# Splits made in place in the output stage, identity products on TensorE at the start of stages, and another order of loads and roundings in an encoder block on one Trainium2 core

## The reference

```python
ada = silu(c) @ w_ada + b_ada                     # six vectors of 1024
u = x * (1 + sc1) + sh1
p_h, p_qkv, p_gate = split(u @ w_in)              # one projection, 1024 -> 5888
y_h = hyena_mixer(p_h, ...)                       # long convolution by transforms
y_a = attention_mixer(p_qkv, positions)           # 3 dilations x 4 heads x 64
gate_h, gate_a = split(sigmoid(p_gate))
merged = gate_h * (y_h @ w_branch_hyena) + gate_a * (y_a @ w_branch_attn)
x = layer_norm(alpha * x + (1 + g1) * (merged @ w_out))
u2 = x * (1 + sc2) + sh2
f = peer(u2, wq, keys, utab, vtab)                # 8 heads, 16384 experts, best 16 per head
x = layer_norm(alpha * x + (1 + g2) * f)
```

## Time and profile before

| | |
|---|---|
| median of 3 runs | 3749.43 us (3746.46 to 3751.86) |
| the profiled execution's own time | 3747.55 us |
| its span | 3745.7 us |
| TensorE busy | 3526.9 us, 94% of the span |
| VectorE, GpSimd, ScalarE busy | 69%, 35%, 34% |
| mean granted clock of TensorE | .975 of full speed |

### The profile page before, as it was taken

How to read it: one execution, slowest core, us unless ns; L and a number is a source line. 1 busy time by engine, 2 the same in 40 slices (tenths; PEclk the granted TensorE clock), 3 DMA queues, 4 the chain that set the end, 5 groups by cost and what they waited for, 6 DMA issues and landing times. The chain is left out here.

```text
span 3745.7 us, 52511 instructions
## 1 busy us (share of the span) xinstructions
PE 3526.9 (94%) x18656; PEld 3116.3 (83%) x18656; DVE 2593.1 (69%) x5904; ACT 1291.3 (34%) x2645; POOL 1317.8 (35%) x815
## 2 busy tenths in 40 slices
PE   5699899999989799999999999999899999999997
PEld 4599788877767688999999999999788888888886
DVE  6663245435654555899988878888488777778877
ACT  2110232221142312322237888888322222222222
POOL 1232122213312112586652222222145555555532
PEclk9799999999999899999999999999999999999999
DMA  5353322327652223588757999999988888888873
GB/s 208 118 161 99 124 86 86 110 86 264 206 180 85 74 67 109 191 291 271 266 199 244 281 271 291 272 274 282 268 307 301 304 302 301 303 316 307 307 271 118
DMA packets 497846, 805.50 MB, mean 215 GB/s; under 512 B 289318, under 2 KB 304455, under 8 KB 494952
## 3 DMA queue, kind: packets, MB, share of 16 engines
q1 hardware_dynamic: 111432, 351.94, 26.9%
q0 software_dynamic: 85520, 311.47, 23.8%
...
...
## 5 line engine op out<-in xcount | busy, mean ns | idle before, releaser
L2451 POOL DMA_INDIRECT va_rows<-in_vtab,k_pick x256 | 481.2, 1880 | 526.0 <-DVE k_big L2629 403.7
L79 PE MATMUL va_fps<-va_vt_h,va_c_h 128*128 128x512 f32 x1536 | 600.5, 391 | 22.1 <-DVEq L2699 8.9
L80 PE MATMUL va_fps<-va_vt_l,va_c_h 128*128 128x512 f32 x1536 | 599.6, 390 | 0.0
L81 PE MATMUL va_fps<-va_vt_h,va_c_l 128*128 128x512 f32 x1536 | 599.5, 390 | 0.0
L2629 DVE SCALAR_TENSOR_TENSOR k_big<-va_rows,k_dots,k_big 128x1024 f32<-128x1024 f32 x254 | 317.8, 1281 | 73.9 <-DMA va_rows<-in_vtab,k_pick 73.9
L79 PEld LDWEIGHTS va_fps<-va_vt_h,va_c_h 128*128 128x128 f32 x1536 | 289.8, 189 | 83.9 <-DVEq L2699 9.3
L2264 ACT ACTIVATE ga_first<-ga_first,ga_gs 128x128 f16<-128x128 f16 x1152 | 355.9, 392 | 0.0
L81 PEld LDWEIGHTS va_fps<-va_vt_h,va_c_l 128*128 128x128 f32 x1536 | 289.7, 189 | 60.5
L80 PEld LDWEIGHTS va_fps<-va_vt_l,va_c_h 128*128 128x128 f32 x1536 | 289.9, 189 | 59.9
L2542 ACT ACTIVATE va_vt_h<-k_edge 128x1024 fp32r<-128x1024 f32 x128 | 135.5, 1058 | 555.7 <-PE va_fps L81 350.9
L2328 DVE TENSOR_SCALAR ga_second<-ga_iota,k_sel 128x128 f16<-128x128 f16 x768 | 201.0, 265 | 107.0 <-PE ga_ps L2226 85.0
...
## 6 DMA issues: line engine op xcount, KB each, us to landing
k_ut<-in_utab SPq DMA_DIRECT2D x128, 512.0 KB, 4.4
k_edge<-in_vtab SPq DMA_DIRECT2D x128, 512.0 KB
scratch_ahead<-k_gelu_a ACTq DMA_DIRECT2D x128, 384.0 KB, 2.7
k_edge<-scratch_ahead SPq DMA_DIRECT2D x128, 384.0 KB
k_edge<-scratch_gates SPq DMA_DIRECT2D x128, 384.0 KB
...
```

Source lines behind the costliest of these rows:

```text
L79: nc.tensor.matmul(out, w[0], x[0], start=first, stop=False)
L80: nc.tensor.matmul(out, w[0], x[1], start=False, stop=False)
L81: return nc.tensor.matmul(out, w[1], x[0], start=False, stop=last)
L2451: nc.gpsimd.indirect_dma_start(got[:, q % SLOTS_G, :], None, vrows, picked(K, q)).then_inc(got_in[q % SLOTS_G], 16)
```

## The change

- `keep_busy(count)` issues plain float32 products of the identity with itself into a PSUM tile that is overwritten later: 24 at the start of qkv, 16 at the start of mix and 14 at its end, 32 at the start of merge, 9 of out, 12 of values.
- setup: the load of `c` stands earlier in its queue, and the wait for the other small loads stands in spectra on VectorE.
- mix: VectorE, not GpSimd, makes the low part of the first weight tile.
- merge: the loads of weight tile 0 stand ahead of that of `y`, GpSimd rounds the weights as well as subtracting, ScalarE rounds `wo` before the sigmoid, VectorE subtracts `wo` before it gates, `wo` is loaded two tiles ahead, and TensorE waits for four `y` tiles and later for six.
- out: `m_h` and `m_l` live in the memory of `k_u_h` and `k_u_l`. When token tile n is turned, ScalarE rounds it into `k_u_h` over `m_h` of that tile, and VectorE subtracts three rows later. VectorE makes `m_l` of tile 0, GpSimd the other seven. There are three row buffers and two of statistics, the roots run two tiles ahead, and rows are stored from SP's queue. The first query weights are loaded here.
- query: no splits of `u2`. VectorE makes the low part of the first weights. `k_u_h` and `k_u_l` are laid out by token tile, so a moving operand is read as four runs of 128 (three in the 384-column products).

The diff, cut to its core (of the products, the forms in query and select stand for the others):

```diff
+def keep_busy(nc, out, K, count):
+
+    for _ in range(count):
+        nc.tensor.matmul(out, K["ident"][:, :], K["ident"][:, :], start=True, stop=True)
...
+            keep_busy(nc, tps[:, 0, 0:P], K, 24)
...
                 nc.gpsimd.tensor_copy(w_h[:, c % 2, :, :], w[:, :, :]).then_inc(w_hi, 1)
+                if c == 0:
+                    continue
                 pool.wait_ge(w_hi, c + 1)
+                pool.wait_ge(w_ok, c)
                 nc.gpsimd.tensor_tensor(w_l[:, c % 2, :, :], w[:, :, :], w_h[:, c % 2, :, :].bitcast(F32),
                                         ALU.subtract).then_inc(w_ok, 1)
...
+            keep_busy(nc, tps[:, 0, 0:P], K, 16)
             for m in lead:
                 project(m)
...
+            keep_busy(nc, sps[:, 0, 0:P], K, 14)
...
+            dve.wait_ge(w_hi, 1)
+            v.tensor_tensor(w_l[:, 0, :, :], w[:, :, :], w_h[:, 0, :, :].bitcast(F32), ALU.subtract).then_inc(w_ok, 1)
...
+            load_w(0)
             sp.dma_start(K["ya"], S["ya"]).then_inc(ya_in, 16)
-            with sp.Fori(0, KT // 2) as i:
-                for s in range(2):
-                    n = 2 * i + s
-                    sp.wait_ge(w_ok, n + 1)
-                    sp.dma_start(w[:, s, 0:NH, :], T["w_bh"][bass.ds(n, 1)][0]).then_inc(w_in[s], 16)
-                    sp.dma_start(w[:, s, NH:NY, :], T["w_ba"][bass.ds(n, 1)][0]).then_inc(w_in[s], 16)
-                    sp.wait_ge(m_ok, n + 1)
-                    sp.dma_start(gate[:, s, 0, :], S["cm"][bass.ds(HY_TILES + n, 1)][0]).then_inc(g_in[s], 16)
-                    sp.dma_start(gate[:, s, 1, :], S["cm"][bass.ds(HY_TILES + KT + n, 1)][0]).then_inc(g_in[s], 16)
-                    sp.wait_ge(wo_lo, n + 1)
-                    sp.dma_start(wo[:, s, :], T["w_out"][:, bass.ds(n, 1), :][:, 0, :]).then_inc(wo_in[s], 16)
+            load_w(1)
+            load_gate(0)
+            load_wo(0)
+            load_gate(1)
+            load_wo(1)
+            for n in range(2, KT):
+                load_wo(n)
+                load_w(n)
+                load_gate(n)
...
-            pool.sem_inc(w_ok, 2)
-            with pool.Fori(0, KT // 2) as i:
-                for s in range(2):
-                    pool.wait_ge(w_hi, 2 * i + s + 1)
-                    nc.gpsimd.tensor_tensor(w_l[:, s, :, :], w[:, s, :, :], w_h[:, s, :, :].bitcast(F32),
-                                            ALU.subtract).then_inc(w_ok, 1)
+            for n in range(KT):
+                pool.wait_ge(w_in[n % 2], 32 * (n // 2 + 1))
+                if n >= 2:
+                    pool.wait_ge(mm, 2 * n + 2)
+                nc.gpsimd.tensor_copy(w_h[:, n % 2, :, :], w[:, n % 2, :, :]).then_inc(w_hi, 1)
+                pool.wait_ge(w_hi, n + 1)
+                nc.gpsimd.tensor_tensor(w_l[:, n % 2, :, :], w[:, n % 2, :, :], w_h[:, n % 2, :, :].bitcast(F32),
+                                        ALU.subtract).then_inc(w_ok, 1)
...
+            keep_busy(nc, ps[:, 0, 0:P], K, 32)
...
                     for a, (lo, hi) in enumerate(((0, NH), (NH, NY))):
+                        pe.wait_ge(y_lo, hi)
...
-                    act.wait_ge(w_in[s], 32 * (i + 1))
-                    act.wait_ge(mm, 2 * n + 2)
-                    nc.scalar.activation(w_h[:, s, :, :], w[:, s, :, :], ACT.Copy).then_inc(w_hi, 1)
+                    act.wait_ge(wo_in[s], 16 * (i + 1))
+                    nc.scalar.activation(K["wo_h"][:, bass.ds(n, 1), :][:, 0, :], wo[:, s, :], ACT.Copy).then_inc(wo_hi, 1)
                     act.wait_ge(g_in[s], 32 * (i + 1))
                     nc.scalar.activation(gate[:, s, :, :], gate[:, s, :, :], ACT.Sigmoid).then_inc(g_ok, 1)
-                    act.wait_ge(wo_in[s], 16 * (i + 1))
-                    nc.scalar.activation(K["wo_h"][:, bass.ds(n, 1), :][:, 0, :], wo[:, s, :], ACT.Copy).then_inc(wo_hi, 1)
...
+                    dve.wait_ge(wo_hi, n + 1)
+                    v.tensor_tensor(K["wo_l"][:, bass.ds(n, 1), :][:, 0, :], wo[:, s, :],
+                                    K["wo_h"][:, bass.ds(n, 1), :][:, 0, :].bitcast(F32), ALU.subtract).then_inc(wo_lo, 1)
...
-                    dve.wait_ge(wo_hi, n + 1)
-                    v.tensor_tensor(K["wo_l"][:, bass.ds(n, 1), :][:, 0, :], wo[:, s, :],
-                                    K["wo_h"][:, bass.ds(n, 1), :][:, 0, :].bitcast(F32), ALU.subtract).then_inc(wo_lo, 1)
...
-        m_h, m_l = sb("m_h", [P, KT, KT, P], F32R), sb("m_l", [P, KT, KT, P], F32R)
+        m_h, m_l = K["u_h"], K["u_l"]
+        u_h, u_l = K["u_h"], K["u_l"]
...
-        x, row = sb("x", [P, 2, D]), sb("row", [P, 2, D])
-        stats = sb("stats", [P, 16])
+        x, row = sb("x", [P, 2, D]), sb("row", [P, ROWS, D])
+        stats = sb("stats", [P, 2, 16])
...
+            sp.dma_start(K["wq"][:, :, :], T["wq"][0]).then_inc(K["wq_in"][0], 16)
+            for n in range(KT):
+                if n + 2 < KT:
+                    load_x(n + 2)
+                sp.wait_ge(row_ok, n + 1)
+                sp.dma_start(rows(S["x1"], n), row[:, n % ROWS, :]).then_inc(stored[n % ROWS], 16)
...
+            for n in range(1, KT):
                 pool.wait_ge(m_hi, n + 1)
+                pool.wait_ge(m_lo, n)
                 nc.gpsimd.tensor_tensor(m_l[:, n, :, :], K["merged"][:, :, tokens(n)], m_h[:, n, :, :].bitcast(F32),
                                         ALU.subtract).then_inc(m_lo, 1)
...
+            keep_busy(nc, tps[:, 0, 0:P], K, 9)
...
+                act.wait_ge(var_ok, n + 1)
+                nc.scalar.activation(stats[:, n % 2, 14:15], stats[:, n % 2, 13:14], ACT.Sqrt).then_inc(root_ok, 1)
+
...
-                act.wait_ge(var_ok, n + 1)
-                nc.scalar.activation(stats[:, 14:15], stats[:, 13:14], ACT.Sqrt).then_inc(root_ok, 1)
-                act.wait_ge(row_ok, n + 1)
-                act.dma_start(rows(S["x1"], n), row[:, s, :]).then_inc(stored[s], 16)
+                if n + 2 < KT:
+                    root(n + 2)
...
                 last.then_inc(u_ok, 1)
-            for s in range(2):
-                act.wait_ge(stored[s], 16 * (KT // 2 + 1))
+                act.wait_ge(u_ok, n + 3)
+                nc.scalar.activation(u_h[:, n, :, :], K["u2"][:, :, tokens(n)], ACT.Copy).then_inc(u_hi, 1)
...
+            dve.wait_ge(m_hi, 1)
+            v.tensor_tensor(m_l[:, 0, :, :], K["merged"][:, :, tokens(0)], m_h[:, 0, :, :].bitcast(F32),
+                            ALU.subtract).then_inc(m_lo, 1)
...
+            def low(n):
+                dve.wait_ge(u_hi, n + 1)
+                v.tensor_tensor(u_l[:, n, :, :], K["u2"][:, :, tokens(n)], u_h[:, n, :, :].bitcast(F32),
+                                ALU.subtract).then_inc(u_lo, 1)
...
-                dve.wait_ge(turned, n + 1)
-                dve.wait_ge(stored[s], 16 * (n // 2 + 1))
+                if n >= ROWS:
+                    dve.wait_ge(turned, n + 3 - ROWS)
+                    dve.wait_ge(stored[n % ROWS], 16 * (n // ROWS))
...
+                if n >= 3:
+                    low(n - 3)
+            for n in range(KT - 3, KT):
+                low(n)
...
-        w = sb("w", [P, 2, KT, P])
+        w = [K["wq"], sb("w", [P, KT, P])]
+        seen = lambda t, k, cut: t[:, cut.start // P:cut.stop // P, k, :]
+        by_tile = lambda t: t.rearrange("p (a b) -> p a b", b=P)
...
-            with sp.Fori(0, HP // 2) as i:
+            sp.dma_start(w[1][:, :, :], T["wq"][1]).then_inc(w_in[1], 16)
...
+            weight_low(1, 1)
...
-                    if first:
-                        pe.wait_ge(u_lo, KT * (h + 1))
                     for k in range(KT):
-                        last = product3(nc, qps[:, 2 * s + h, :], (w_h[:, s, k, :], w_l[:, s, k, :]),
-                                        (u_h[:, k, cut], u_l[:, k, cut]), k == 0, k == KT - 1)
+                        last = product3(nc, by_tile(qps[:, 2 * s + h, :]), (w_h[:, s, k, :], w_l[:, s, k, :]),
+                                        (seen(u_h, k, cut), seen(u_l, k, cut)), k == 0, k == KT - 1)
...
-            for h in range(2):
-                cut = slice(h * HALF, (h + 1) * HALF)
-                for k in range(KT):
-                    nc.scalar.activation(u_h[:, k, cut], K["u2"][:, k, cut], ACT.Copy).then_inc(u_hi, 1)
-                    if (h, k) == (0, KT // 2):
-                        high(0, 0, 0)
+            high(0, 0, 0)
...
-                    v.tensor_tensor(u_l[:, k, cut], K["u2"][:, k, cut], u_h[:, k, cut].bitcast(F32), ALU.subtract).then_inc(u_lo, 1)
+            dve.wait_ge(w_hi, 1)
+            v.tensor_tensor(w_l[:, 0, :, :], w[0][:, :, :], w_h[:, 0, :, :].bitcast(F32), ALU.subtract).then_inc(w_ok, 1)
...
-                        last = product3(nc, aps[:, 2 * (a % 2) + h, 0:DH], (ut_h[split_of(a)][:, k, :], ut_l[split_of(a)][:, k, :]),
-                                        (u_h[:, k, cut], u_l[:, k, cut]), k == 0, k == KT - 1)
```

(7 more changed lines are left out.)

114 lines of the change are left out of this document (70 added, 44 removed).

## The result

The changed kernel takes 3730.49 us (median of 5 runs, 3726.86 to 3730.75) against 3749.43 (median of 5, 3744.82 to 3751.86). The ratio is 0.995, with a 95% interval of 0.9939 to 0.9961: 18.9 us less, by the interval 15 to 23. The forecast was 3728, range 3717 to 3738. The profiled execution's span fell from 3745.7 to 3728.7, by 16.9.

A forecast was written before the change was run, and what follows sets the result against it. TensorE, busy in 94% of the span, was taken to bound the kernel. Terms 3.35 + 4.2 + 2.8 + 1.4 + 9.2 = 21.0 us, giving a median of 3728.4 us, range 3717 to 3738.

The forecast's parts named there:

- qkv 0, hyena 0, values 0: Stages qkv, hyena and values: no gain counted; hyena 0 to 1.5, values' early win waited off at a later split.
- Mix 3.35: Mix: start 0.95 us earlier plus 2.4 from first products at full clock; 3.35 us (2.5 to 3.5).
- Merge start 4.2: Merge's start: first product 1.9 us earlier, behind the identities, plus 2.2 of clock; 4.2 us (2.0 to 6.2).
- 2.4 back: Mix's first products: slow-clock loss, taken as like those of merge and query, recovered; 2.4 us.
- in merge itself the products are dense, and GpSimd's added rounding hides under them: Inside merge: GpSimd's extra rounding, about a microsecond per tile of 7.8 us, costs TensorE nothing.
- Merge end and out start 2.8: Merge's end and out's start: 1.6 us from an earlier start plus 1.2 of clock; 2.8 us (1.9 to 4.1).
- Out end 1.4: Out's end: roots two tiles ahead let VectorE take the last row earlier, ScalarE finishing late; 1.4 us (0.5 to 1.8).
- Query start 6.65 and 2.55 of clock: Query's start: no split between transposes and products gains 6.65 us, most cold loss saved; together 9.2 us (7.5 to 9.9).
- Rival 1: Identities don't raise the clock but hold TensorE at half speed; gain 6.9 us, time 3742.5; chance 0.08.
- Rival 2: Identities stay at full clock from the start, hyena and values gain too; gain 26 to 28 us, 3722; chance 0.14.
- Rival 3: Query, select, gates: moving operand in runs of 128 slows 6,912 matmuls; 3763 us at 5 ns each; chance 0.05.
- Rival 4: Out: new waits for row buffers and low parts lengthen each of eight turns; time near 3735 us; chance 0.03.

The follow-up runs named there:

- in_place_only: Kernel before with only the changed out and query stages, token-tile layout and its readers, and output weights at the far end; no identities: 3738.28 us, ratio 0.9971.
- no_ident: Changed kernel with every keep_busy call taken out: 3729.44 us, ratio to before 0.9951.
- ident_on_before: Kernel before with the same six groups of identity products and nothing else: 3739.67 us, ratio 0.9977.
- combined: Changed kernel with branch weights loaded ahead of output weights in merge, output weights 192 bytes lower, fewer identities: 3727.03 us; the same without any identities: 3732.34.
- wo_right: Kernel before with both output weight tiles at the far end of SBUF: 3754.03 us.
- m_right: Kernel before with m_h and m_l at the far end of SBUF, output weights where they were: 3751.49 us.
- merge_w_ahead: Changed kernel with branch weights loaded ahead of output weights in merge from tile 2 on: one time, 3728.80 us.

## Why the prediction was right, term by term

The forecast of 21.0 us is 2.1 more than the medians show and inside the interval. The pieces tell more: those that the sum spoke of (mix, merge, out, query) moved by 14.8, and the other 2.1 of the span's 16.9 came from pieces that it held at 0, spectra's 2.0 first of all. So it was right in sign and size, with three terms too large, and its closeness is in part luck: the pieces that it priced fell 6.2 us short of 21.0. Of that the pieces held at 0 gave back 2.1, and another 2.0 comes from the executions that were profiled, 1.9 us below its median for the kernel before and 0.1 above it for the changed one. The two ways of winning were not equally borne out. The edits of out and query alone bring 10.1 us (in_place_only). The identities were to bring 5.8 of clock (2.4, 2.2 and 1.2 in mix, merge and out), and in the changed kernel as it stands no run can tell them from nothing (no_ident); that they work is shown by ident_on_before (8.4) and by the pair of combined (5.3).

- **qkv 0, hyena 0, values 0**: right in this pair. -0.2; +0.4 and -0.8; +1.3 and -1.5. In values the 12 identities outlast the 3.0 us that the low part needs after the barrier, and a later wait takes that back, as the term said; by the trace it is that for VectorE's `k_big`, not ScalarE's split. The fourteen at mix's end do nothing. Qkv is less sure: the seven kernels with the 24 identities take 248.9 to 249.9 us there, of the seven without three take 251.0 to 251.5 and show a stretch at 0.50 at 206 to 208 us. Whether the 24 keep that stretch away is open.
- **Mix 3.35**: 1.9. The start came 1.03 earlier (0.95 forecast), though not by the identities' end: they were through at 413.99, and TensorE waited 0.60 us more for VectorE's low part. The products won 0.9 and not 2.4. The step that failed is "2.4 back": the kernel before had no second slow stretch in mix, the changed one has it at 430.3, nine products in 3.4 us where 15 would fit at full clock, about 1.4 us. Whether the change brings it is open. All eight kernels with the changed mix show such a stretch, at 430.2 to 434.8, with or without identities; of the six with the mix stage of before only wo_right and m_right do, at 436 and 435. So the term is 2.4 less what that stretch costs.
- **Merge start 4.2**: start 1.98 (1.9 forecast), and for the reason given, the identities end last. The rows:

```profile
1044.11 1.16 POOL L1405 CAST me_w_h<-me_w 128x768 fp32r<-128x768 f32 x1 [24.88 <-DMA me_w<-in_w_ba]
1045.35 2.67 POOL L1407 TENSOR_TENSOR me_w_l<-me_w,me_w_h 128x768 fp32r<-128x768 f32 x1
...
1065.17 2.67 POOL L1407 TENSOR_TENSOR me_w_l<-me_w,me_w_h 128x768 fp32r<-128x768 f32 x1
...
1042.22 6.88 DVE L1450 TENSOR_TENSOR me_y_l<-k_big,me_y_h 128x1024 fp32r<-128x1024 f32 x4 [1.96 <-ACT me_y_h L1433]
...
1044.50 1.84 DVE L1450 TENSOR_TENSOR me_y_l<-k_big,me_y_h 128x1024 fp32r<-128x1024 f32 x1
...
1046.27 2.83 DVE L1450 TENSOR_TENSOR me_y_l<-k_big,me_y_h 128x1024 fp32r<-128x1024 f32 x1
...
1041.30 8.98 PE L87 MATMUL me_ps<-k_ident 128*128 128x128 f32 x64 [4.67 <-PEq L96]
1050.04 0.48 PE L79 MATMUL me_ps<-me_y_h,me_w_h 128*128 128x512 f32 x1
```

32 of them last from 1041.30 to the product at 1050.04, 8.7 us, as estimated, against 1049.10 for the fourth low part of `y` and 1048.02 for GpSimd's. The four low parts took 6.88 us together, where four of the earlier trace rows would take 4.7, so the 1 us allowed for both engines at once was 2.2. The single instructions (the third and fourth of the four are shown by themselves) tell how. The first two, before GpSimd began, took 1.23 and 1.22. The third ends 1.07 behind the end of GpSimd's copy (1045.27), GpSimd's subtraction 1.68 behind the end of that third one (1046.34), and the fourth 1.08 behind the end of the subtraction (1048.02). These ends are those of engines that take turns: each instruction is long by what it waits for the other's. The clock won 2.2 (65.6 for 67.7 in merge_w_ahead), but 1.5 of it was lost again. The step that failed is "in merge itself the products are dense, and GpSimd's added rounding hides under them": it was argued from the rounding's length, and the new order of the loads in SyncE's queue was not followed past tile 1.
- **Merge end and out start 2.8**: -0.7, from 1.0 at the start, 0.8 of clock, and then 2.5 lost. The rows:

```profile
1122.17 1.23 DVE L1604 TENSOR_TENSOR k_u_l<-k_big,k_u_h 128x1024 fp32r<-128x1024 f32 x1 [2.41 <-ACT k_u_h L1576]
...
1121.03 4.18 PE L87 MATMUL ou_tps<-k_ident 128*128 128x128 f32 x18 [3.88 <-PEq L96]
1124.86 0.77 PE L79 MATMUL ou_ps<-k_wo_h,k_u_h 128*128 128x512 f32 x1
```

`m_l` of tile 0 was ready at 1123.40, but nine identities, all at half clock, ended with 1124.86; the term took 1.6 for the start although the upper of its own two values for the identities, 3.8 us, leaves only 1.0. The 2.5 us (384 products at 6.4 ns more) follows the distance between the operands, of which nothing in the forecast speaks. It had named runs of 128 elements as the danger to TensorE's step, and the danger sat in where the allocator put a tile.
- **Out end 1.4**: 1.8. **Query start 6.65 and 2.55 of clock**: 7.0 and 2.2. The rows:

```profile
1219.93 1.22 DVE L1620 TENSOR_TENSOR ou_row<-ou_ps,k_ada_row 128x1024 f32<-128x1024 f32 x1 [3.42 <-PE ou_ps L81]
...
1236.28 1.23 DVE L1610 TENSOR_TENSOR k_u_l<-k_big,k_u_h 128x1024 fp32r<-128x1024 f32 x1 [2.65 <-ACT k_u_h L1596]
...
1235.19 1.06 ACT L1596 ACTIVATE k_u_h<-k_big 128x1024 fp32r<-128x1024 f32 x1
...
1238.80 3.65 PE L1729 MATMUL qu_sps<-k_ident,k_big 128*128 128x128 f32 x16 [9.31 <-PEq L96]
1242.10 0.72 PE L79 MATMUL qu_qps<-k_u_h,qu_w_h 128*128 128x512 f32 x1
```

VectorE takes up row 7 at 1219.93, right behind the last product (1219.49 + 0.40 = 1219.89), and not 6.8 us later. ScalarE's last split ends at 1236.25, VectorE's low part at 1237.51, and query's transposes start at 1238.80: the chain of ScalarE that the prediction wrote out. Then nothing stands between transposes and product. This is the largest term and the best worked out, because every piece of it had a row.

**Rivals.** Rival 1 (identities hold TensorE at half speed) is excluded by the windows: 1.00 in mix and merge. (Its own terms, 1.4 + 6.65 + 1.3 - 2.8, make 6.6 and not 6.9; nothing hangs on it.) Rival 2 (identities at full clock from the start) is excluded too: merge's clock was 0.50 until 1044.6, 3.3 us into the identities, and out's nine all ran at 0.50. A shadow of rival 1 is true, that in out, where only nine fit and the clock was at 0.50 through all of them, they cost 1.4 and bring 0.6 (products of 95.41 us without them in no_ident, 94.85 with). Rival 3 (runs of 128) is excluded: the groups of the kernel before and of the changed one read

```profile
L79 PE MATMUL ga_aps<-k_u_h,k_ut_h 128*128 128x384 f32 x752 | 259.9, 346 | 3.8 <-ACTq L2233 3.8
...
L79 PE MATMUL se_aps<-k_u_h,k_ut_h 128*128 128x384 f32 x592 | 199.0, 336 | 1.0 <-POOL k_ut_l L1914 0.9
```

```profile
L79 PE MATMUL ga_aps<-k_u_h,k_ut_h 128*128 128x384 f32 x752 | 260.0, 346 | 3.9 <-ACTq L2298 3.9
...
L79 PE MATMUL se_aps<-k_u_h,k_ut_h 128*128 128x384 f32 x592 | 199.5, 337 | 1.4 <-POOL k_ut_l L1977 1.4
```

346 ns for 346, 337 for 336, and a step of 173 ns in both; query's step of 512 columns, read in four runs, has a median of 227 ns in both. The rule of the Trainium skill in "PSUM — Partial Sum Buffer", Specifications (TRN2), that a non-contiguous access pattern slows matmuls significantly, is not contradicted, since the PSUM side was contiguous, but for a moving operand in SBUF read in runs of 512 bytes no run here shows a price. The other rule weighed, "TensorE: Matmul & The Clock Gate", Part 4, on transposes and the full clock, is contradicted by the earlier trace rows and does not fit here either: between the barrier and query's first product TensorE ran only transposes, and the window behind them has 0.95, which leaves about 0.6 us at half clock. Rival 4 did not occur: out's turns are TensorE's, 12.1 us each, of which 0.3 is the slower step.

What stays open: why the distance between the operands acts, whether its modulus is 256 or 512 bytes, and what values between those four give; and how much of the 2.0 us in spectra is the moved wait of the setup stage. It was not tried alone, and the piece scatters by as much without it. The edits of mix (VectorE's low part) and merge (order, roundings) were not tried alone either: in_place_only and no_ident differ by them and the setup's, and are 10.1 and 18.7 us below their kernels before, with the traces giving 1.2 us at mix's start and 3.0 at merge's.
